# Second input projection: twelve of its fourteen tiles as six pairs of seven half-size products

## The chip, the cores and the metric

The kernel runs on one core of a Trainium2 chip. The metric is the device time of one execution in microseconds (us). The engines are PE (TensorE: matmuls), DVE (VectorE), ACT (ScalarE), POOL (GpSimd) and SP (SyncE, which here only starts DMA transfers). Each works through its own list of instructions in order, and they wait for one another by semaphores.

## The reference, cut to what matters

A first block (gated convolutions, a feed-forward part) turns `x`, 1024 tokens by 1024 channels, into the input of a second block. This one projects the normalised input `h` to 1984 columns `u`, and these feed a latent attention and a multiscale pool:

```python
h = _rms(x, norm_g[l]) * (1.0 + scale[:, None, :]) + shift[:, None, :]
hc = _rms(ctx, norm_g[l]) * (1.0 + scale_c) + shift_c
u = h @ w_in[l]            # 1024 x 1984
uc = hc @ w_in[l]
...
cq = u[..., OFF_CQ:OFF_CKV]        # 256 columns
ckv = u[..., OFF_CKV:OFF_KR]       # 128
k_rope = u[..., OFF_KR:OFF_GA]     # 64
gate_a = u[..., OFF_GA:OFF_PIN]    # 512
pool_in = u[..., OFF_PIN:OFF_GP]   # 512
gate_p = u[..., OFF_GP:D_IN_PROJ]  # 512
...
br_a = jax.nn.silu(gate_a) * mla_out
br_p = jax.nn.silu(gate_p) * _multiscale_pool(pool_in, w_pool, pool_scale)
y = jnp.concatenate([br_a, br_p], axis=-1) @ w_out[l]
```

`_multiscale_pool` takes four groups of 128 channels with windows of 2, 4, 8 and 16 tokens: window mean minus the value, times a 128x128 matrix per group (`w_pool`), times `pool_scale`. The attention has four heads; `cq` and `ckv` are normalised over their columns before they are expanded into queries, keys and values.

## The kernel before

Every float32 matmul is made as three products of shorter operands: each factor is split into a high part and the low rest, and high·high, high·low and low·high are summed. For weights, the high copy comes from ACT or POOL and the rest from a POOL subtraction; for the activations, ACT writes `XBh` (`xb_hi` in the rows) and DVE `XBl` (`xb_lo`).

A plain `gemm` (L963) of a column tile of 128 has 8 slices of the inner dimension, 3 products and 2 halves of 512 tokens: 48 matmuls 128x512. The second input projection uses it for its 14 full tiles after the key columns. The first input projection (L1108), the up-projection (L1251) and the output (L1638) already use another scheme: a pair of tiles, cut into halves in all three dimensions, is computed by seven products of half size instead of eight, with sums and differences of weight quarters and of token quarters as operands. One product has 4 slices times 3 products: 12 matmuls of 128x512. In the up-projection the rows call the token combinations `tok_comb`, the weight sums `w_sums` (DVE), the high copies `whi` (ACT, L1956) and the low parts `wlo` (POOL, L879). In the output, ACT copies a product's bank (`out_copies`, L2270) and DVE adds another to it (L3199).

The order on PE in the stage: context keys and rotary keys; keys (`key_tile`, interleaved with the DVE loop that makes `hT` and `XBl`, while ACT makes `XBh`, L2091); two query tiles; four tiles of gate a, with `row_sums` of the squared keys (L1029) inside the second and `column_sums` of the squared queries (L1020) inside the fourth; four tiles of pool input (`pin`); then four times a tile of gate p and a pooled product with `w_pool` (6 matmuls); then the heads (L1399 on). ACT evicts each tile (squares and copies of the queries L2104 and L2105, SiLU of the gates L2115 and L2129) and builds the scales with a logarithm and an exponential (L1711, L1717), each behind a table load. DVE writes the block's residual `y` (8 pieces; SP stores them to DRAM as `y_scratch`), the low parts of keys and queries, the rotary keys, and the pool sums (L2982 to L2997); a helper `pool_low` writes the low half of a pooled operand. ACT starts four DMAs that swap rotary halves (`U3`).

The lists of instructions are fixed in the program; no planner rearranges them.

## Time and profile before

| | |
|---|---|
| median of 3 runs | 1904.87 us (1903.58 to 1905.76) |
| profiled execution, span of the trace | 1904.2 us |
| granted TensorE clock over the span, share of full | 0.998 |
| PE busy | 1864.6 us (98%), 8807 matmul instructions |
| DVE / ACT / POOL busy | 1397.6 / 733.7 / 906.7 us |
| DMA | 166.63 MB, 88 GB/s on average |

The profiled execution has one span, which is compared with spans; the runs are timed without a profile. "Busy" is time in which an engine executes; matmuls are pipelined, so a busy PE can still be slower than its best. The positions in the rows are microseconds from the start of the span.

### The profile page before, as it was taken

To read this page: it belongs to the slowest core of one execution; us is meant where nothing else is said; L and a number is where in the kernel's file an instruction comes from. 1 tells how busy PE (TensorE), PEld (TensorE's weight loads), DVE (VectorE), ACT (ScalarE), POOL (GpSimd) and SP (SyncE) were. 2 spreads that over 40 slices of the span, in tenths; PEclk is the share of its full clock that TensorE was granted. 3 is DMA by queue.
4 is the path that set the end of the run, shared out by engine and by line. 5 is a ranking of instruction groups with operands and counts; after the bars stand their busy time and mean duration, and the time that the engine had idled before them with its cause. 6 is when DMAs were issued, how large, how long until landed. Compare 5 with 4: busy or idle time off the path is not lost.

```text
span 1904.2 us, 23795 instructions
## 1 busy us (share of the span) xinstructions
PE 1864.6 (98%) x8807; PEld 1544.8 (81%) x8807; DVE 1397.6 (73%) x1423; ACT 733.7 (39%) x990; POOL 906.7 (48%) x632
## 2 busy tenths in 40 slices
PE   7999999999999999999999999999999999999998
PEld 6788888778888888888887788878788878888887
DVE  7989988667348889898989786574633846667683
ACT  5433344441225333333341200243433236766643
POOL 5866766533334555555566555332233521222462
PEclk9999999999999999999999999999999999999999
DMA  4112234356112323232336435111123210000052
GB/s 164 52 45 89 67 111 144 122 177 187 45 45 66 100 67 99 66 99 66 99 136 232 146 106 198 56 41 38 45 82 112 84 45 1 12 12 1 1 177 67
DMA packets 190952, 166.63 MB, mean 88 GB/s; under 512 B 11267, under 2 KB 168912, under 8 KB 190864
## 3 DMA queue, kind: packets, MB, share of 16 engines
q1 hardware_dynamic: 189536, 162.82, 27.0%
...
## 4 chain that ended last, share of the span: by engine, by line
PE 84%; DVE 8%; ACT 3%; issue 2%; DMA 1%; POOL 1%; ACTq 0%; SPq 0%; DVEq 0%
PE ps L963 33%; PE ps L1251 19%; PE ps L1108 16%; PE ps L1638 3%; PE ps L1454 2%; PE ps L1489 1%; PE ps L1487 1%; PE ps L1488 1%; PE ps L1468 1%; PE ps L1465 1%; PE ps L1471 1%; PE ps L1474 1%; PE ps L1462 1%; DVE resid L2707 1%; DVE mod_acc L2410 1%
## 5 line engine op out<-in xcount | busy, mean ns | idle before, releaser
L833 POOL TENSOR_TENSOR small<-ones 128x1 f32<-128x1 f32 x75 | 22.2, 296 | 479.0 <-PE ps L963 438.7
L963 PE MATMUL ps<-xb_hi,whi 128*128 128x512 f32 x752 | 244.6, 393 | 5.1 <-DVE resid L2707 2.3
L963 PE MATMUL ps<-xb_lo,whi 128*128 128x512 f32 x752 | 242.2, 389 | 0.0
L963 PE MATMUL ps<-xb_hi,wlo 128*128 128x512 f32 x752 | 242.0, 389 | 0.0
L838 POOL TENSOR_TENSOR wlo<-raw,whi 128x1024 fp32r<-128x1024 f32 (+1 forms) x72 | 197.4, 2742 | 6.0
L879 POOL TENSOR_TENSOR wlo<-w_sums,whi 128x512 fp32r<-128x512 f32 x80 | 138.1, 1745 | 82.3 <-ACT whi L1956 82.3
L963 PEld LDWEIGHTS ps<-xb_hi,whi 128*128 128x128 f32 x752 | 140.2, 188 | 38.0 <-DVE resid L2707 3.1
L963 PEld LDWEIGHTS ps<-xb_lo,whi 128*128 128x128 f32 x752 | 141.2, 188 | 29.7 <-issue 0.2
L963 PEld LDWEIGHTS ps<-xb_hi,wlo 128*128 128x128 f32 x752 | 141.2, 188 | 29.6
L2390 DVE SCALAR_TENSOR_TENSOR ps<-glu_pad,tab,ps 128x1024 f32<-128x1024 f32 x116 | 149.2, 1286 | 2.9
L933 POOL TENSOR_SCALAR prob<-prob,small 128x512 f32<-128x512 f32 x64 | 50.5, 802 | 180.8 <-DVE small L3045 180.2
L1251 PE MATMUL ps<-tok_comb_hi,whi 128*128 128x512 f32 x320 | 124.5, 389 | 0.0
L1251 PE MATMUL ps<-tok_comb_lo,whi 128*128 128x512 f32 x320 | 124.5, 389 | 0.0
L1251 PE MATMUL ps<-tok_comb_hi,wlo 128*128 128x512 f32 x320 | 124.5, 389 | 0.0
L858 POOL TENSOR_TENSOR wlo<-w_in_sums,whi 128x512 fp32r<-128x512 f32 x64 | 88.2, 1381 | 58.5 <-ACT whi L1803 58.5
L963 PE MATMUL ps<-xa_hi,whi 128*128 128x512 f32 x352 | 113.5, 396 | 1.7 <-DVE resid L2707 0.8
L963 PE MATMUL ps<-xa_lo,whi 128*128 128x512 f32 x352 | 111.2, 390 | 0.0
L963 PE MATMUL ps<-xa_hi,wlo 128*128 128x512 f32 x352 | 111.1, 390 | 0.0
L1108 PE MATMUL ps<-xb_hi,whi 128*128 128x512 f32 x272 | 106.3, 391 | 1.5 <-DVE xb_lo L2424 0.9
L1108 PE MATMUL ps<-xb_hi,wlo 128*128 128x512 f32 x272 | 105.8, 389 | 0.0
L1108 PE MATMUL ps<-xb_lo,whi 128*128 128x512 f32 x272 | 105.8, 389 | 0.0
L2707 DVE TENSOR_TENSOR resid<-ps,resid 128x1024 f32<-128x1024 f32 x48 | 58.5, 1219 | 55.7 <-PE ps L963 55.6
...
## 6 DMA issues: line engine op xcount, KB each, us to landing
...
```

Source lines behind the costliest of these rows:

```text
L833: nc.gpsimd.tensor_tensor(small[:, 106 + slab.slot:107 + slab.slot], ones[:, 0:1], ones[:, 0:1], ALU.mult)
L838: nc.gpsimd.tensor_tensor(lo, src, f32(hi), ALU.subtract).then_inc(split_done, 1)
L858: nc.gpsimd.tensor_tensor(wlo[:, slot, cols], win_source(p, k), f32(whi[:, slot, cols]), ALU.subtract).then_inc(sem("win_split"), 1)
L879: nc.gpsimd.tensor_tensor(wlo[:, s, cols], comb_source(u, n), f32(whi[:, s, cols]), ALU.subtract).then_inc(sem("st_split"), 1)
L933: nc.gpsimd.tensor_scalar(Pr[t % 2][:, k], Pr[t % 2][:, k], rsum4[:, t % 4:t % 4 + 1], 0.0, ALU.mult, ALU.add).then_inc(sem("p_scaled"), 1)
L963: ins = mm(dst[j], w, r[j], start=first and f, stop=last and l)
L1108: last = mm(o, wp[:, slot, w], bp[:, k0 + j, c0:c0 + H], start=k in (1, 2, 5) and j == 0 and i == 0, stop=j == 3 and i == 2, skip_group_ch ...
L1251: last = mm(o, wp[:, s, w], bp[:, k, :], start=k == 0 and i == 0, stop=k == 3 and i == 2)
L1454: last = nc.tensor.transpose(PS[:, o:o + P], Pr[a][:, k * P:(k + 1) * P], ident[:, :])
L1638: last = mm(o, wp[:, slot, w], bp[:, k0 + j, c0:c0 + H], start=k in (1, 2, 5) and j == 0 and i == 0, stop=j == 3 and i == 2, skip_group_ch ...
L2390: stt(conv_ps if k < TAPS_A - 1 else conv[:, i, :], source, col("conv_a_w", i + 4 * k), conv_ps, ALU.mult, ALU.add).then_inc(sem("conv_tap ...
L2707: tt(R[:, m, :], pair(J), R[:, m, :], ALU.add).then_inc(*one(free(J)))
```

## The change

Two tiles of the pool input (pooling groups 3 and 2) stay plain gemms. The other twelve are made as six pairs of seven products: pair 0 the two other pool-input tiles, 1 and 2 gate a, 3 the queries, 4 and 5 gate p. `UP_AT` is the order of the 42 products; product 1 of the next pair stands between product 7 and product 4 of a pair. The weights go through a ring of four half slots: ACT's high copy (`u_hi`) waits for the product four earlier, POOL's subtraction (`u_split`) for the copy.

Around it work is dealt anew. ACT also writes `hfull`, the full-precision activations (8 copies in the h loop), from which DVE makes four token combinations in place and, with ACT's high copies (`comb_hi`), their low parts (`comb_low`). Rotary keys and the low part of `KSQ` move from DVE to POOL; the `U3` DMAs move from ACT's queue to SP's. `row_sums` moves into the first remaining pool-input tile, `column_sums` behind product (4,7). The four pooled products stand behind the products in `POOLED_AFTER`; ACT scales their results, and they are stored to DRAM and read back (`pool_results`). The gates of pairs 1 and 2 are stored and read back as `ga` (2 MB) at the end. The slabs, jobs and buffers of the old order are replaced, among them the mean and scale helpers. VectorE waits for all y stores (`y_out`) before it zeroes the pads of the pool buffers. The pooled branch ends with `branch_gate`, `branch_high` and `branch_low`, two of each per gate pair; those of pair 5 come in head 0.

```diff
+NUP = 6
+UP_AT = {(0, 1): 0}
+for _p in range(NUP):
+    for _k in (2, 6, 5, 7):
+        UP_AT[_p, _k] = len(UP_AT)
+    if _p + 1 < NUP:
+        UP_AT[_p + 1, 1] = len(UP_AT)
+    for _k in (4, 3):
+        UP_AT[_p, _k] = len(UP_AT)
+UP_PRODUCTS = len(UP_AT)
+UP_OF = {g: pk for pk, g in UP_AT.items()}
+PIN_PAIR, CQ_PAIR = 0, 3
+GATE_P = {4: (2, 3), 5: (0, 1)}
+POOLED_AFTER = {(1, 5): 0, (1, 3): 1, (2, 3): 2, (3, 7): 3}
...
+        JK = Lin(JOBS["mla_in"] + 3)
+        sp.wait_ge(sem("rbc_ready"), 5)
+        sp.dma_start(inv[:, :], A["inv_cnt"][GROUPS[0]:GROUPS[0] + 1, :].to_broadcast([P, S])).then_inc(sem("inv_in"), 16)
+        sp.wait_ge(*free(JK))
+        for half in (0, 32):
+            for u in range(2):
+                sp.dma_start(U3[ROPE + half + 16 * u:ROPE + half + 16 * (u + 1), 0:S],
+                             krT[half + 16 * (1 - u):half + 16 * (2 - u), 0:S]).then_inc(sem("rope_in"), 16)
...
         for m in range(8):
+            if m == 4:
+                sp.wait_ge(split_done, SLABS["pin"] + 2)
+                u_load(0)
             sp.wait_ge(sem("y_ready"), m + 1)
             sp.dma_start(ydram[m], R[:, m, :]).then_inc(sem("y_out"), 16)
-        L = Lin(SLABS["pin"])
-        for n, gq in enumerate(GROUPS):
-            slab8(L + n, w2, OFF_PIN + gq * P)
...
-        for n, gq in enumerate(GROUPS):
-            slab8(Lin(SLABS["pool"] + n), w2, OFF_GP + gq * P)
+        sp.wait_ge(job_done, JOBS["pin"] + 2)
+        u_load(1)
...
+        sp.wait_ge(*on("u_done", UP_AT[NUP - 1, 7] + 1))
+        sp.wait_ge(*on("ga_out", 64))
+        sp.dma_start(ga[:, :, :], gdram[0:4].rearrange("t p n -> p t n")).then_inc(sem("ga_in"), 16)
+        sp.wait_ge(*on("u_done", UP_PRODUCTS))
         sp.dma_start(csq[:, :], A["rope_q"]).then_inc(sem("rope_in"), 16)
...
+                pool.wait_ge(sem("rope_in"), 96)
+                nc.gpsimd.tensor_tensor(ktmp[:, :], U3[ROPE:P, 0:S], cossin[ROPE:P, :], ALU.mult).then_inc(sem("krot_mul"), 1)
+                pool.wait_ge(sem("krot_mul"), 1)
+                nc.gpsimd.tensor_tensor(krT[:, 0:S], krT[:, 0:S], cossin[0:ROPE, :], ALU.mult).then_inc(sem("krot_done"), 1)
+                pool.wait_ge(sem("krot_done"), 1)
+                nc.gpsimd.tensor_tensor(krT[:, 0:S], krT[:, 0:S], ktmp[:, :], ALU.add).then_inc(sem("krot_done"), 1)
+                for g in range(UP_PRODUCTS):
+                    slot, cols = u_ring(g)
+                    pool.wait_ge(*on("u_hi", g + 1))
+                    nc.gpsimd.tensor_tensor(wlo[:, slot, cols], u_source(*UP_OF[g]), f32(whi[:, slot, cols]),
+                                            ALU.subtract).then_inc(sem("u_split"), 1)
+                    if UP_OF[g] == (0, 7):
+                        pool.wait_ge(*on("u_split", g + 1))
+                        pool.wait_ge(sem("ksq_hi"), 1)
+                        nc.gpsimd.tensor_tensor(KSQ[ROPE:P, :], sqkr[:, :], f32(KSQ[0:ROPE, :]), ALU.subtract).then_inc(sem("ksq_low"), 1)
+                        pool.wait_ge(*on("ksq_low", 1))
...
             if n == 2:
+                pe.wait_ge(*free(Lin(JOBS["mla_in"] + 3)))
+                row_sums(sqck, NKEY, sem("lora_sq"), 3, SQ_AT)
...
+        J = Lin(JOBS["pin"])
+        L = Lin(SLABS["pin"])
+        gemm(J, L, XBh, XBl, KD, w8, between=lora_sums)
+        pe.wait_ge(sem("ck_f"), 1)
+        gemm(J + 1, L + 1, XBh, XBl, KD, w8)
+
+        def u_product(p, k):
+
+            g, o = UP_AT[p, k], u_bank(p, k)
+            slot, cols = u_ring(g)
+            pe.wait_ge(*on("u_split", g + 1))
+            if p == 0 and k in HX:
+                pe.wait_ge(*on("hx_dve", 4 + HX_LOW.index(k) + 1))
+            if (p, k) == (0, 1):
+                pe.wait_ge(*free(J))
+            if (p, k) == (0, 5):
+                pe.wait_ge(*free(J + 1))
+            if k == 1 and p >= 2:
+                pe.wait_ge(*on("u_act", up_acts(p - 2, 1)))
+            if k == 2 and p >= 2:
+                pe.wait_ge(*on("u_add", 3 * p - 5))
+            if k == 5 and p >= 2:
+                pe.wait_ge(*on("u_add", 3 * p - 3))
+            if k in (6, 7, 4):
+                pe.wait_ge(*on("u_copy", 3 * p + {6: 1, 7: 2, 4: 3}[k]))
+            if k == 3:
+                pe.wait_ge(*on("u_add", 3 * p + 2))
...
+            last.then_inc(sem("u_done"), 1)
+
+        for p, k in UP_AT:
+            u_product(p, k)
+            if (p, k) in POOLED_AFTER:
+                pooled_product(POOLED_AFTER[p, k])
+            if (p, k) == (4, 7):
+                pe.wait_ge(*on("wp_read", 4))
+                column_sums(pres[0], 8, 16, sem("s12_done"), 23)
...
+        pe.wait_ge(*on("u_add", 3 * NUP - 3))
+        pe.wait_ge(*on("u_act", up_acts(NUP - 2, 1)))
...
+            fn(hfull[:, m, :], hT[:, m, :], ACT.Identity, bias=mod_sb[:, m, 0:1]).then_inc(sem("h_hi"), 1)
+        row_log(rbc, D, 6, 0, S, at_col=6 * H)
+        row_scale(PS[:, 6 * H:6 * H + S], rbc[:, :]).then_inc(sem("rbc_ready"), 1)
+
+        def comb_hi(k):
+
+            b, k0, c0 = HX[k]
+            act.wait_ge(*on("hx_dve", HX_ORDER.index(k) + 1))
+            fn(xch[:, b, :, :], hfull[:, k0:k0 + 4, c0:c0 + H], ACT.Copy).then_inc(sem("hx_hi"), 1)
+
         keys_out(J + 2, 0, S)
+        comb_hi(5)
         rope_out(J + 3, 0, S)
-        act.wait_ge(*free(J + 3))
-        for half in (0, 32):
-            for u in range(2):
-                act.dma_start(U3[half + 16 * u:half + 16 * (u + 1), 0:S],
-                              krT[half + 16 * (1 - u):half + 16 * (2 - u), 0:S]).then_inc(sem("rope_in"), 16)
...
+        row_log(sqck, 128, 7, 0, NKEY, at_col=SQ_AT)
+        row_scale(PS[:, SQ_AT:SQ_AT + NKEY], sqck[:, :]).then_inc(sem("rbc_ready"), 1)
...
+        def u_hi(g):
+
+            if g >= UP_PRODUCTS:
+                return
+            p, k = UP_OF[g]
+            slot, cols = u_ring(g)
+            if g < 4:
+                act.wait_ge(job_done, JOBS["pin"] + 1 + g // 2)
+            else:
+                act.wait_ge(*on("u_done", g - 2 if g in (UP_PRODUCTS - 3, UP_PRODUCTS - 1) else g - 3))
+            if k in (1, 2, 4):
+                u_raw_in(act, p)
+            else:
+                act.wait_ge(*on("u_sum", 4 * p + {5: 1, 6: 2, 7: 3, 3: 4}[k]))
+            fn(whi[:, slot, cols], u_source(p, k), ACT.Copy).then_inc(sem("u_hi"), 1)
+
+        def u_copy(p, n):
+
+            k, to = ((1, upc[p % 2][:, 0:H]), (6, upc[p % 2][:, H:S]), (7, upd[p % 2][:, H:S]))[n]
+            if n == 0 and p in (3, 4):
+                act.wait_ge(*on("ga_out", 32 * (p - 2)))
+            elif n == 0 and p == 5:
+                act.wait_ge(sem("cq_lo"), 2)
+                act.wait_ge(sem("lora_sq"), 6)
...
+            act.wait_ge(*on("u_done", UP_AT[p, k] + 1))
+            fn(to, u_bank(p, k), ACT.Copy).then_inc(sem("u_copy"), 1)
...
+        for p in range(NUP):
+            b = 7 * p + 1
+            if p:
+                u_hi(b + 4)
+                if p == 3:
+                    pooled_high(3)
+                if p == 5:
+                    root(8, 1)
+                u_copy(p, 1)
+            u_hi(b + 5)
+            u_hi(b + 6)
+            if p == 1:
+                pooled_out(0)
+            u_copy(p, 2)
+            if p == 3:
+                pooled_out(3)
+            u_hi(b + 7)
+            if p in (1, 2):
+                pooled_high(p)
+                inverse_counts(p + 1)
+                if p == 1:
+                    pool_in(3)
+            if p + 1 < NUP:
+                u_copy(p + 1, 0)
+                u_hi(b + 8)
+                u_hi(b + 9)
             else:
...
+                branch_high(4, 0)
+                branch_high(4, 1)
+            u_last_block(p)
+            u_hi(b + 10)
+            if p in (1, 2):
+                pooled_out(p)
+            if p == 4:
+                act.wait_ge(*on("wp_out", 64))
+                fn(CKh[:, :], ckf[:, :], ACT.Copy).then_inc(sem("ck_hi"), 1)
+            if p:
+                u_finish(p)
+            else:
+                pooled_high(0)
+                inverse_counts(1)
+                pool_in(2)
...
-                dve.wait_ge(sem("h_hi"), m)
+                dve.wait_ge(sem("h_hi"), 2 * m)
...
+        u_sums(0, (1,))
+        combination(3)
+        comb_low(6)
+        comb_low(5)
+        u_sums(0, (3,))
+        comb_low(7)
+        comb_low(4)
...
+        pool_sums(0, 0, 3)
+        for p in range(NUP):
+            u_add(p, upc[p % 2][:, 0:H], 2, 1)
+            if p == 1:
+                pool_sums(1, 2, 3)
+                pool_means(1)
+            if p == 4:
+                for k in (1, 0):
+                    dve.wait_ge(*on("u_act", up_acts(CQ_PAIR, 3 - k)))
+                    stt(CQl[:, k, :], (upc, upd)[k][CQ_PAIR % 2][:, :], col("q_lora_g_2", k), f32(CQh[:, k, :]),
+                        ALU.mult, ALU.subtract).then_inc(sem("cq_lo"), 1)
+                dve.wait_ge(sem("lora_sq"), 6)
+                tt(pres[0][:, :], pres[0][:, :], pres[1][:, :], ALU.add).then_inc(sem("s12_done"), 1)
+            if p == 5:
+                rstd(8, 256, 1, 1, at_col=16, to=rql)
+                branch_gate(4, 0)
+                branch_gate(4, 1)
+            u_add(p, upd[p % 2][:, H:S], 5, 3)
+            u_sums(p + 1, (1,))
+            if p == 0:
+                pool_sums(0, 3, 4)
+                pool_means(0)
+            if p == 5:
+                dve.wait_ge(sem("ck_hi"), 2)
+                tt(CKl[:, :], ckf[:, :], f32(CKh[:, :]), ALU.subtract).then_inc(sem("ck_lo"), 1)
+                branch_low(4, 0)
+                branch_low(4, 1)
+            if p in (1, 2, 3):
+                pool_low(p)
+            u_add(p, upc[p % 2][:, H:S], 3, 2)
+            u_sums(p + 1, (3,))
+            if p == 0:
+                pool_low(0)
+                pool_sums(1, 0, 2)
+            if p in (1, 2):
+                pool_sums(p + 1, 0, GROUPS[p + 1] + 1)
+                pool_means(p + 1)
+        branch_gate(5, 0)
+        branch_gate(5, 1)
...
-                pool_low(3)
+                branch_low(5, 0)
+                branch_low(5, 1)
```

## Rows read from the trace of the kernel before

**Rows 1.** Busy time by stretch: PE, PEld, DVE, ACT, POOL, clock, DMA, GB/s
```profile
594.00:990.00 396.00, 396.00 (x1749) 328.01 (x1748) 354.28 (x346) 144.37 (x203) 228.10 (x144) 1.00 0.28 86
1393.00:1558.00 165.00, 163.97 (x724) 133.89 (x723) 78.25 (x56) 40.93 (x39) 65.48 (x49) 1.00 0.29 86
1558.00:1580.00 22.00, 19.68 (x103) 15.35 (x102) 16.79 (x22) 20.76 (x29) 2.48 (x3) 1.00 0.22 55
```

**Rows 2.** Timeline of PE: start, us, engine, line, operation, tiles
```profile
1393.84 0.70 PE L963 MATMUL ps<-xb_hi,whi 128*128 128x512 f32 x2
...
1429.32 2.31 PE L1029 MATMUL ps<-sq_ckv,ones 128*128 128x512 f32 x6
...
1457.75 1.84 PE L1020 MATMUL ps<-ones,sq_cq 128*128 128x1 f32 x16
...
1557.63 0.47 PE L1399 MATMUL ps<-ck_hi,whi 128*128 128x512 f32 x1
```

**Rows 3.** Timeline of ACT, evictions of two tiles (in brackets, idle before)
```profile
1405.04 1.03 ACT L2104 ACTIVATE sq_cq<-ps 128x1024 f32<-128x1024 f32 x1 [9.20 <-PE ps L963]
...
1415.92 1.03 ACT L2104 ACTIVATE sq_cq<-ps 128x1024 f32<-128x1024 f32 x1 [8.94 <-PE ps L963]
```

**Rows 4.** Waits of PE's weight loads, 1390 to 1560: us in total, times, longest
```profile
PEld ps L963 <- ACT silu_gate_p L2129: 1.6, 3, 1.3
```

**Rows 5.** Chain of waits, 1550 to 1582: start, us, what ran
```profile
1556.35 1.03 ACT silu_gate_p L2129
...
1559.85 0.70 ACT kn_hi L2179
...
1579.27 0.50 PE ps L1462
```

**Rows 6.** Operations by tile: shortest/median/longest ns, first to last start in us
```profile
L2645 DVE TENSOR_TENSOR tok_comb<-tok_comb x4: 2292/2948/4308, 575.3 to 593.8; 128x2048 f32<-128x2048 f32 x4
...
L1942 ACT ACTIVATE tok_comb_hi<-tok_comb x4: 1898/1910/1923, 587.2 to 597.1; 128x2048 fp32r<-128x2048 f32 x4
...
L1956 ACT ACTIVATE whi<-w_sums x80: 612/632/635, 608.6 to 979.1; 128x512 fp32r<-128x512 f32 x80
...
L879 POOL TENSOR_TENSOR wlo<-w_sums,whi x80: 1286/1650/2336, 609.3 to 980.2; 128x512 fp32r<-128x512 f32 x80
...
L2691 DVE TENSOR_TENSOR w_sums<-raw x10: 692/1477/1479, 607.1 to 947.5; 128x512 f32<-128x512 f32 x10
...
L2270 ACT ACTIVATE out_copies<-ps x9: 597/598/602, 1836.3 to 1889.2; 128x512 f32<-128x512 f32 x9
...
L3199 DVE TENSOR_TENSOR out_copies<-ps,out_copies x9: 676/684/693, 1847.6 to 1896.6; 128x512 f32<-128x512 f32 x9
...
L2091 ACT ACTIVATE xb_hi<-h_t,mod_sb x8: 1150/1154/1158, 1368.1 to 1383.7; 128x1024 fp32r<-128x1024 f32 x8
```

**Rows 7.** Timeline of ACT, a table load and the operation that it serves
```profile
1440.89 1.28 ACT L1711 ACT_TABLE_LOAD   x1
1442.19 1.33 ACT L1711 ACTIVATE sq_ckv<-ps,small 128x1280 f32<-128x1280 f32 x1
```

**Rows 8.** DMA, 1380 to 1450: GB/s in 40 equal slices
```profile
GB/s 0 0 0 0 0 0 0 0 65 263 108 190 124 0 9 0 0 155 145 0 0 0 0 4 146 405 424 417 414 419 419 324 35 0 0 0 5 0 147 152
```

**Rows 9.** Timeline of DVE around 1501
```profile
1500.45 1.22 DVE L2997 TENSOR_TENSOR xa_lo<-pooled,xa_hi 128x1024 fp32r<-128x1024 f32 x1 [1.13 <-ACT xa_hi L2134]
1501.59 3.43 DVE L2982 TENSOR_TENSOR win_a<-u_pad 128x1039 f32<-128x1039 f32 x1
```

**Rows 10.** Timeline of POOL: one beside that addition, one that began first
```profile
1500.48 3.45 POOL L838 TENSOR_TENSOR wlo<-raw,whi 128x1024 fp32r<-128x1024 f32 x1
...
1534.76 2.40 POOL L838 TENSOR_TENSOR wlo<-raw,whi 128x1024 fp32r<-128x1024 f32 x1
```

**Rows 11.** Timeline of PE near the start of the program
```profile
17.29 1.94 PE L1038 MATMUL ps<-ident,x_scaled 128*128 128x128 f32 x8 [2.35 <-DVE x_scaled L2363]
```

**Rows 12.** Busy time near the start, columns as in rows 1
```profile
17.00:21.00 4.00, 3.71 (x19) 3.71 (x20) 3.52 (x7) 2.97 (x6) 0.00 (x0) 0.57 0.33 130
```

More of the change, by code:

```diff
@@ L56 @@
 for _name, _n in (("glu", 2), ("mix_b", KD // 2), ("mix_a", KD // 2), ("wo", KD),
-                  ("ffn", 4), ("down", 4 * (NDC - 1) + 2), ("ple", KD), ("mla_in", 4), ("ga", 4),
-                  ("pin", 4), ("w_pool", 2), ("pool", 4), ("heads", HEADS), ("out", 2), ("end", 0)):
+                  ("ffn", 4), ("down", 4 * (NDC - 1) + 2), ("ple", KD), ("mla_in", 2),
+                  ("pin", 2), ("heads", HEADS), ("out", 2), ("end", 0)):
     SLABS[_name] = _at
@@ new lines, in u_load, with ga_store @@
+        def u_load(p):
+            first, second = up_columns(p)
+            for r in range(4):
+                c = (first, second)[r // 2]
+                sp.dma_start(u_raw(p, r).rearrange("p (k n) -> p k n", n=P),
+                             w2[H * (r % 2):H * (r % 2 + 1), c:c + P].rearrange("(k p) n -> p k n", p=P)
+                             ).then_inc(sem(f"u_raw{p % 2}"), 16)
+        def ga_store(p):
+            sp.wait_ge(*on("u_act", up_acts(p, 2)))
+            sp.dma_start(gdram[2 * p - 1], upd[p % 2][:, :]).then_inc(sem("ga_out"), 16)
+            sp.wait_ge(*on("u_act", up_acts(p, 3)))
+            sp.dma_start(gdram[2 * p - 2], upc[p % 2][:, :]).then_inc(sem("ga_out"), 16)
@@ L1385, in tensor_program @@
-        gemm(j + 2, L + 2, XBh, XBl, KD, w8)
-        gemm(j + 3, L + 3, XBh, XBl, KD, w8, between=lora_scales)
-        J, L = Lin(JOBS["pin"]), Lin(SLABS["pin"])
-        for gq in range(4):
-            gemm(J + gq, L + gq, XBh, XBl, KD, w8, begins=3 if gq == 2 else 1)
-        J, L = Lin(JOBS["pool"]), Lin(SLABS["pool"])
-        for n, gq in enumerate(GROUPS):
-            gemm(J + 2 * n, L + n, XBh, XBl, KD, w8)
-            pe.wait_ge(sem("branch2_lo"), n + 1)
-            gemm(J + (2 * n + 1), None, XAh[:, 4 + gq:5 + gq, :], XAl[:, 4 + gq:5 + gq, :], 1,
-                 lambda k: (gq, slice(0, P)), new_slab=False, weights=(wpoolh, wpooll))
+                pe.wait_ge(*free(Lin(JOBS["mla_in"] + 3)))
@@ new lines, in u_sums @@
+        def u_sums(p, which):
+            if p >= NUP:
+                return
+            a11, a12, a21, a22 = (u_raw(p, r) for r in range(4))
+            s1, s2, s3, s4 = (u_sum(p, r) for r in range(4))
+            if 1 in which:
+                u_raw_in(dve, p)
+                if p >= 2:
+                    dve.wait_ge(*on("u_split", UP_AT[p - 1, 5] + 1))
+                tt(s1, a21, a22, ALU.add).then_inc(sem("u_sum"), 1)
+                dve.wait_ge(*on("u_sum", 4 * p + 1))
+                tt(s2, s1, a11, ALU.subtract).then_inc(sem("u_sum"), 1)
+            if 3 in which:
+                if p:
+                    dve.wait_ge(*on("u_split", UP_AT[p - 1, 3] + 1))
+                else:
+                    dve.wait_ge(job_done, JOBS["pin"] + 2)
+                tt(s3, a11, a21, ALU.subtract).then_inc(sem("u_sum"), 1)
+                dve.wait_ge(*on("u_sum", 4 * p + 2))
+                tt(s4, a12, s2, ALU.subtract).then_inc(sem("u_sum"), 1)
@@ new lines, in pool_sums @@
+        def pool_sums(n, first, last):
+            u = upad[n % 2]
+            if first == 0:
+                if n:
+                    dve.wait_ge(sem("branch2_lo"), n)
+                if n < 2:
+                    dve.wait_ge(*free(Lin(JOBS["pin"] + n)))
+                else:
+                    dve.wait_ge(*on("u_pin", n - 1))
+            for s in range(first, last):
+                src, dst = u if s == 0 else (wB, wA)[s % 2], (wA, wB)[s % 2]
+                ln = TB // 4 - (1 << (s + 1)) + 1
```

413 lines of the change are left out of this document (253 added, 160 removed).

## The prediction, made before the changed kernel was run

> **What bounds the kernel now.** I read the stretches by engine first. In the stage that the change rewrites TensorE is busy for 163.97 of 165 us, while VectorE has work for 78, ScalarE for 41 and GpSimd for 65 [rows 1]. The up-projection, which already runs seven-product pairs, is bound by TensorE too: 396.00 of 396.00, beside VectorE at 354 and GpSimd at 228 [rows 1]. That row matters twice: it shows that the scheme can hide its helpers, and how much VectorE work that can mean.
>
> Then TensorE's own order of time [rows 2]. The stage runs from 1393.84 (first query gemm) to 1557.63 (first product of the heads), 163.8 us. A plain tile is the distance between two evictions that each wait for a gemm, 1415.92−1405.04 = 10.88 us [rows 3], so one of its 48 matmuls takes 0.2267. Fourteen tiles are 152.3, the four pooled products of six matmuls 4×1.36 = 5.4, row sums 2.31 and column sums 1.84 [rows 2]: 161.9. The other 1.9 us are waits; the list of waits puts 1.6 us of it on the pooled branch's SiLU [rows 4].
>
> Behind the stage, the chain of waits leaves TensorE: from 1556.35 to 1579.27 it runs through ScalarE and VectorE [rows 5], and ScalarE is busy for 20.76 of these 22 us [rows 1]. A delay of head 0's first inputs is paid in full.
>
> **The change part by part.**
>
> *TensorE's work.* Twelve tiles go (130.6 us), 42 products of twelve matmuls come (42×2.72 = 114.2). Row sums, column sums and pooled products stay. **−16.3.** The waits of the old order go with it: **−1.9** (bounds −1.9 and 0).
>
> *Entry.* ScalarE gets eight more copies (hfull) in the loop over m. The two ScalarE operations take 2×1.15 plus about 0.04 of handoff = 2.34 per m; the loop now advances every 2.23 (1368.1 to 1383.7, seven steps) [rows 6]. The copy before XBl's wait also delays XBl of m = 0 by 1.15, some of which the key tiles were already waiting for. I take **+0.8**, seven times the 0.11; bounds 0.3 and 1.5.
>
> *Row sums moved forward.* In the first remaining tile (pin 0) they wait for rope_out on ScalarE, which now stands behind the longer h loop, two log/exp steps with a 1.28 us table load each [rows 7], the key outputs and one comb_hi of 1.9 [rows 6]. Added up from the before-trace's positions: done about 1398.3; TensorE is there at 1397.3. **+1.0** (0.5 to 1.5). Then the row scale is ready about 1407.6, before pin 0 ends at 1408.6: no second wait.
>
> *Pairs 0 to 2.* Pair 0 starts when pin 1 ends, near 1419.5. It needs token combinations and their low halves from VectorE, which first waits until all eight y stores have landed. 4 MB at 419 GB/s is 10 us [rows 8]; starting about 1400, behind the rotary copies now on SP, they land near 1415.5. VectorE then does two weight sums, combination 3 and the lows, to about 1422.4, 1425.2, 1429.8 and 1432.5; products 6, 5, 7 and 4 are due at 1425.0, 1427.7, 1430.4 and 1435.8. So all are in time with at least 0.6 to spare for product 7, and y landing has about 2.5 us of slack before anything is late. Small waits for product 3's sum and two pooled products: 0.2+0.6+0.5 = **+1.3**, bounds 0 and 6. Here the row that speaks against the change is that of VectorE and GpSimd together: an addition of 1.2 us took 3.43 beside a GpSimd subtraction that took 3.45 instead of 2.40 [rows 9, 10], that is, they ran one after the other. Fully serial, the stretch costs 9.1 us more (a rival below); I stay near the low end because the up-projection has the same mix of engines without a wait of TensorE [rows 1]. The Trainium skill, page "GPSIMD Engine Reference", section "8. Key points", states that GpSimd shares its SBUF interfaces with VectorE, with contention when a VectorE instruction has two SBUF inputs; by that rule the serial sum holds wherever both are queued, and these two rows agree with it.
>
> *Pooled product 3.* It stands right after (3,7) and needs pool_low(3). On VectorE that is behind u_add(3,5), which needs ScalarE's copy of product 7's bank, taken after (3,7) ends, and behind two weight sums. So TensorE waits: drain 0.16, copy 0.60, add 0.68, two sums at 0.69, pool_low 1.22, three handoffs of 0.06: 0.16+0.60+0.68+1.38+1.22+0.18 = **+4.2** [rows 6, 9]. If the two sums meet GpSimd they take 1.48 each [rows 6]: 5.8; below, 3.9 if drain and handoffs vanish.
>
> *Last pair.* No product of a next pair lies between (5,7) and (5,4). (5,7) waits for a copy that on ScalarE stands behind the CKh copy, pair 4's SiLUs, a weight copy and a square-root table load of 1.28 [rows 7]; (5,4) waits for drain, copy and handoff (0.16+0.60+0.12 = 0.9 [rows 6]). **+1.8** (0.9 to 2.5).
>
> *Head 0's entry.* Before, the last SiLU (1.03) began 1.28 ahead of the first head product and KNh began 2.22 after it [rows 2, 5]. Now the last product is followed by drain 0.16, add 0.68, SiLU 1.03, the two KRs copies 2.45 and four handoffs of 0.05: KNh at +4.5, so 2.3 later. On VectorE there is also one more pool low-half (1.2 [rows 9]) in this chain; the second high-half copy runs while VectorE leads. **+3.5** (2.3 to 5).
>
> *Costed at nothing.* Weight loads of 256 KB: 419 GB/s [rows 8] brings a pair's 1 MB in 2.5 us of its 19. Storing the gates and reloading 2 MB at the end: 5 us, and the first use is some 7 us after the last product; without that cover it costs what is late. KSQ and rotary operations on GpSimd: 7 splits of 1.3 to 1.65 per pair [rows 6] leave it over 7 of 19 us; uncovered, each is a delay of the ring. Squares and CQl of pair 3 are done about 1.8 us before the column sums need them.
>
> Sum: −16.3 −1.9 +0.8 +1.0 +1.3 +4.2 +1.8 +3.5 = −5.6. The profiled span of 1904.2 becomes 1898.6. The median of the runs is 1904.87, 0.7 above that span; I carry this over: **1899.3**. All low bounds together give −9.3, all high bounds +6.0.
>
> **Rivals.**
>
> *Serial VectorE and GpSimd.* Suppose that no VectorE operation overlaps a GpSimd one. From the y landing to pooled product 0 (due about 1449.5) VectorE has a combination and four lows of 128x2048 at no less than 2.3 (11.5), four sums at 0.69 (2.8), nine pool operations at 1.22 (11.0) and three adds at 0.68 (2.0): 27.3 [rows 6, 9]. GpSimd has seven splits at 1.29 (9.0) and, estimated by element count from these, 5 for KSQ and w_pool: 14.0. That is 41.3 in 34.1 us: +7.2. Pair 1: eight pool operations, four sums, three adds and seven splits make 23.6 against seven products and a pooled one, 20.4: +3.2. Of these 10.4, 1.3 is counted: 1899.3+9.1 = 1908.4. For: the two rows [rows 9, 10]. Against: the up-projection [rows 1], and that much of this work is needed later than it is queued.
>
> *The clock falls at pooled product 3.* Early in the program TensorE idled 2.35 us [rows 11], and over the next 4 us the granted clock was 0.57 [rows 12], near the lower of its two levels (1.2 of 2.4 GHz): 0.43×4 = 1.7 us lost. The wait of 4.2 is longer than that gap: 1901.0. Against: this gap followed no long busy stretch. The Trainium skill, page "TensorE: Matmul & The Clock Gate", section "HAM oscillation — how this bites in real kernels", has the clock fall in idle gaps between groups of matmuls; rows 12 agree.
>
> *The ring starves: slower.* With four half slots, a weight copy waits for the product four back, and ScalarE takes its work strictly in order, so a copy stuck behind a SiLU or a branch wait holds the next product. 42 products: 0.13 us each takes the whole gain, 0.22 each makes it slower by over 0.2%. One product's time lost in each pair is 6×2.72 = 16.3: 1915.6. For: ScalarE's queue here carries pool inputs, gates and pooled results that the up-projection's lacks. Against: a copy of 0.63 per 2.72 us product [rows 6] leaves three products of lead.
>
> *The waits are hidden.* If VectorE runs ahead of this count at pooled product 3 (−4.2) and the tail copies are early (−1.8): 1893.3.
>
> **How the numbers follow.** A measurement here tells about 0.2% from no change, 3.8 us. Chances: the forecast 0.50 (its own range 1895.6 to 1904), serial 0.15, clock 0.13, ring 0.08, hidden 0.14. Faster by over 0.2% means under 1901.1: 0.36 of the forecast, half the clock's (0.06), all of hidden (0.14): 0.56. Slower means over 1908.7: 0.04 of the forecast, 0.08 of serial, 0.01 of clock, 0.07 of ring: 0.20. Same: 0.24. The range goes from 1893 (hidden) to 1909 (just past serial); ring and the edges lie outside, about 0.2.
>
> **What would show it.** Right: products 2.72 apart in the pairs; one wait of about 4 us before the pooled product behind (3,7), released by VectorE; waits near 0.9 at (5,7) and (5,4); KNh 4 to 5 us after the first head product; y landed near 1415.5. Wrong: weight-load waits on GpSimd's splits throughout (ring), VectorE additions of 3 us in pairs 0 and 1 (serial), a granted clock below 1 in pair 4 (clock), y landing after 1418 (each further us costs one), or a chain in head 0 that hides the late KNh.

## The result, and the profile after

The changed kernel takes 1910.88 us (median of 8 runs, 1909.24 to 1912.34); the kernel before took 1905.22 beside it. The ratio is 1.003, 95% interval 1.002 to 1.004: slower by 5.7 us, where 5.6 us faster was forecast, and just above the range (1909). The profiled execution has a span of 1910.2 us, 6.0 above that of before, so it shows the loss. TensorE executes 72 matmuls fewer, as the change says.

The stretches first (columns as in [rows 1]):

```profile
1393.00:1558.00 165.00, 153.09 (x653) 123.25 (x652) 119.77 (x95) 84.02 (x110) 98.78 (x54) 0.97 0.40 127
1420.00:1445.00 25.00, 19.10 (x71) 14.37 (x70) 24.86 (x14) 10.97 (x15) 21.20 (x9) 0.86 0.19 53
1558.00:1580.00 22.00, 17.45 (x80) 13.35 (x80) 20.43 (x22) 19.68 (x26) 3.30 (x3) 0.95 0.41 127
```

TensorE is busy for 153 of these 165 us instead of 164. About half of what is missing lies in the 25 us of pair 0, where VectorE is busy throughout (24.86) and GpSimd nearly so (21.20), and where the granted clock is 0.86. TensorE's own waits, from its timeline (start, us, engine, line, operation; in brackets the idle time before and who ended it):

```profile
1397.47 2.40 PE L1171 MATMUL ps<-sq_ckv,ones 128*128 128x512 f32 x6
...
1427.59 0.47 PE L1565 MATMUL ps<-h_comb_hi,whi 128*128 128x512 f32 x1 [0.29 <-issue]
...
1432.08 0.50 PE L1565 MATMUL ps<-h_comb_hi,whi 128*128 128x512 f32 x1 [1.49 <-POOL wlo L1055]
...
1439.21 0.79 PE L1565 MATMUL ps<-xb_hi,whi 128*128 128x512 f32 x1 [4.12 <-POOL wlo L1055]
...
1468.63 0.47 PE L1565 MATMUL ps<-xb_hi,whi 128*128 128x512 f32 x1 [0.78 <-DVE u_second L3351]
...
1508.26 0.70 PE L1105 MATMUL ps<-pooled_hi,w_pool_hi 128*128 128x512 f32 x2 [3.92 <-issue]
...
1549.19 0.47 PE L1565 MATMUL ps<-h_comb_hi,whi 128*128 128x512 f32 x1 [0.54 <-ACT u_first L2355]
...
1552.93 0.47 PE L1565 MATMUL ps<-h_comb_hi,whi 128*128 128x512 f32 x1 [0.78 <-ACT u_second L2355]
...
1558.50 0.39 PE L1578 MATMUL ps<-ck_hi,whi 128*128 128x512 f32 x1
```

The last row is the first product of the heads, at 1557.63 before [rows 2]. The first remaining pool-input tile begins at 1394.75, so the stage takes 163.75 us, where its old form takes 163.79 from the first query gemm: the work that TensorE saves is lost again in the stage. The waits stand before products (0,5), (0,7) and (1,1), product (1,3), pooled product 3, and (5,7) and (5,4) of the last pair. The granted clock behind the two long ones, and in head 0 (0.50 is the lower of its two levels, 1.2 of 2.4 GHz):

```profile
1437.00:1439.00 2.00, 0.00 (x0) 0.00 (x0) 1.97 (x2) 0.00 (x0) 1.98 (x1) 0.66 0.00 0
1439.00:1444.00 5.00, 4.79 (x11) 3.79 (x12) 4.93 (x5) 0.00 (x0) 4.92 (x4) 0.50 0.00 0
1509.00:1513.00 4.00, 4.00 (x12) 3.09 (x11) 0.00 (x0) 1.74 (x2) 0.41 (x1) 0.57 0.20 81
1576.00:1582.00 6.00, 4.72 (x26) 4.60 (x26) 3.26 (x6) 5.97 (x9) 0.00 (x0) 0.72 0.00 0
```

So each of the two long waits is paid again: 0.50×5 = 2.5 us behind the one of 4.12, 0.43×4 = 1.7 behind the one of 3.92. In head 0 the fall costs nothing that the profile shows: ScalarE and VectorE lead there. Two rows of ScalarE, before and after:

```profile
1571.17 1.47 ACT L2215 ACTIVATE k_scale_bc<-ps,small 128x256 f32<-128x256 f32 x2
```

```profile
1575.76 1.47 ACT L2508 ACTIVATE k_scale_bc<-ps,small 128x256 f32<-128x256 f32 x2
```

This operation begins 13.54 us behind the first head product before and 17.26 after, 3.72 later. The first turned probabilities come 28.89 behind it before (at 1586.52) and 32.61 after (at 1591.11), also 3.72 later. So the whole delay is there before the clock falls, at about 1577.

What makes pair 0 wait is seen where VectorE and GpSimd are put side by side. First VectorE, then GpSimd, timelines:

```profile
1420.81 6.68 DVE L3262 TENSOR_TENSOR xa_lo<-h_full,h_comb_hi 128x2048 fp32r<-128x2048 f32 x2
1427.42 0.68 DVE L3288 TENSOR_TENSOR w_sums<-raw 128x512 f32<-128x512 f32 x1
...
1428.62 5.55 DVE L3262 TENSOR_TENSOR xa_lo<-h_full,h_comb_hi 128x2048 fp32r<-128x2048 f32 x2
1434.10 3.94 DVE L3306 TENSOR_TENSOR win_a<-u_pad 128x1039 f32<-128x1039 f32 x1
1438.07 2.18 DVE L3306 TENSOR_TENSOR win_b<-win_a 128x1037 f32<-128x1037 f32 x1
```

```profile
1419.68 5.66 POOL L1055 TENSOR_TENSOR wlo<-u_sums,whi 128x512 fp32r<-128x512 f32 x2 [4.00 <-ACT whi L2338]
1428.90 3.13 POOL L1055 TENSOR_TENSOR wlo<-w_sums,whi 128x512 fp32r<-128x512 f32 x1 [3.56 <-ACT whi L2338]
1432.10 4.84 POOL L1060 TENSOR_TENSOR k_rope_squares<-sq_kr,k_rope_squares 64x1280 fp32r<-64x1280 f32 x1
1437.02 2.14 POOL L1055 TENSOR_TENSOR wlo<-w_raw,whi 128x512 fp32r<-128x512 f32 x1
```

Two splits that take 1.29 each at their shortest [rows 6] take 5.66 together beside low halves; the low halves, 2.28 at their shortest, take 6.68 for two. The rotary squares, 2.92 where they begin first (e5), take 4.84: they end 2.8 us after the last low half, which ends at 1434.17. The addition at 1434.10, 1.2 alone [rows 9], takes 3.94: it ends 1.1 us after the rotary squares end at 1436.94. GpSimd's list has the split of (0,7), the rotary squares and the split of (1,1) one behind the other, and that is the wait of 4.12. The busy columns contain this waiting of one engine for the other; the rows show it as length and not as idle time. An addition of VectorE with one operand in PSUM (the memory of the matmul results, `ps` in the rows) does not wait in this way. Two of VectorE, then one of GpSimd:

```profile
1443.12 0.68 DVE L3351 TENSOR_TENSOR u_second<-ps,u_second 128x512 f32<-128x512 f32 x1
1443.72 1.15 DVE L3280 TENSOR_TENSOR w_sums<-w_raw 128x512 f32<-128x512 f32 x1
```

```profile
1443.04 1.28 POOL L1066 TENSOR_TENSOR w_pool_lo<-w_pool_raw,w_pool_hi 128x512 fp32r<-128x512 f32 x1
```

The first has one operand in PSUM and keeps its 0.68 beside GpSimd's 1.28. The weight sum has both in SBUF, the on-chip memory of the other tiles; it takes 1.15 and ends 0.55 after GpSimd's operation, which ends at 1444.32.

### The profile page after: what moved, and what is told of

Its sections match the earlier page's. It is cut to its first block, busy times and chain, and to the rows that moved or that the text cites. A ratio compares the mean times of both kernels' runs of the same rounds, so it can differ in the third digit from the quotient of the medians.

```text
span 1910.2 us, 23874 instructions
## 1 busy us (share of the span) xinstructions
PE 1857.0 (97%) x8735; PEld 1536.5 (80%) x8735; DVE 1447.6 (76%) x1466; ACT 787.0 (41%) x1071; POOL 936.4 (49%) x637
## 4 chain that ended last, share of the span: by engine, by line
PE 83%; DVE 9%; issue 3%; ACT 2%; DMA 1%; POOL 1%; SPq 0%; ACTq 0%; DVEq 0%; POOLq 0%
PE ps L1105 28%; PE ps L1393 19%; PE ps L1250 16%; PE ps L1565 4%; PE ps L1820 3%; PE ps L1634 2%; PE ps L1667 1%; PE ps L1669 1%; PE ps L1668 1%; PE ps L1642 1%; PE ps L1645 1%; PE ps L1648 1%; PE ps L1654 1%; PE ps L1651 1%; DVE resid L3000 1%
## 5 line engine op out<-in xcount | busy, mean ns | idle before, releaser
L957 POOL TENSOR_TENSOR small<-ones 128x1 f32<-128x1 f32 x61 | 15.6, 255 | 387.0 <-PE ps L1105 354.2
L1105 PE MATMUL ps<-xb_hi,whi 128*128 128x512 f32 x560 | 185.0, 393 | 4.9 <-DVE resid L3000 2.3
L1105 PE MATMUL ps<-xb_lo,whi 128*128 128x512 f32 x560 | 183.0, 389 | 0.0
L1105 PE MATMUL ps<-xb_hi,wlo 128*128 128x512 f32 x560 | 182.9, 389 | 0.0
L962 POOL TENSOR_TENSOR wlo<-raw,whi 128x1024 fp32r<-128x1024 f32 (+2 forms) x59 | 161.8, 2742 | 4.9
L1105 PEld LDWEIGHTS ps<-xb_hi,whi 128*128 128x128 f32 x560 | 104.5, 188 | 29.4 <-issue 3.7
L1105 PEld LDWEIGHTS ps<-xb_lo,whi 128*128 128x128 f32 x560 | 105.1, 188 | 22.2 <-issue 0.2
L1105 PEld LDWEIGHTS ps<-xb_hi,wlo 128*128 128x128 f32 x560 | 105.1, 188 | 22.0
L982 POOL TENSOR_TENSOR wlo<-w_in_sums,whi 128x512 fp32r<-128x512 f32 x64 | 88.2, 1380 | 59.2 <-ACT whi L1985 59.2
L1250 PE MATMUL ps<-xb_hi,whi 128*128 128x512 f32 x272 | 106.3, 391 | 0.9 <-DVE xb_lo L2717 0.9
L1250 PE MATMUL ps<-xb_hi,wlo 128*128 128x512 f32 x272 | 105.8, 389 | 0.0
L1250 PE MATMUL ps<-xb_lo,whi 128*128 128x512 f32 x272 | 105.8, 389 | 0.0
```

The lines of the kernel that those rows point to most:

```text
L962: nc.gpsimd.tensor_tensor(lo, src, f32(hi), ALU.subtract).then_inc(split_done, 1)
L982: nc.gpsimd.tensor_tensor(wlo[:, slot, cols], win_source(p, k), f32(whi[:, slot, cols]), ALU.subtract).then_inc(sem("win_split"), 1)
L1105: ins = mm(dst[j], w, r[j], start=first and f, stop=last and l)
L1250: last = mm(o, wp[:, slot, w], bp[:, k0 + j, c0:c0 + H], start=k in (1, 2, 5) and j == 0 and i == 0, stop=j == 3 and i == 2, skip_group_ch ...
```

## Experiments

Ratios are to the kernel before, run beside each; the changed kernel's own is 1.003. An interval is 0.001 to 0.0015 (1.9 to 2.9 us) to either side. In profiles I compare the stretch from the row sums to the first head product: what lies ahead of the stage moves by up to 3.7 us from one profile to the next, without a change there.

### e1: rotary squares earlier on GpSimd

```diff
         comb_hi(6)
+        act.wait_ge(sem("krot_done"), 2)
+        act.wait_ge(sem("lora_sq"), 4)
+        fn(KSQ[0:ROPE, :], sqkr[:, :], ACT.Copy).then_inc(sem("ksq_hi"), 1)
         pool_in(0)
...
-                    if UP_OF[g] == (0, 7):
+                    if UP_OF[g] == (0, 2):
```

> Edit: the rotary squares' high copy on ScalarE moves up behind the third token copy, and GpSimd's low half of it from behind the split of product (0,7) to behind the split of (0,2), where GpSimd has 4 us without work. Theory (a long operation in the split queue at the wrong place): the 4.12 us wait of TensorE before product (1,1) goes, and with it the stretch of half clock behind it (about 2.5 us); a wait of about 0.5 us for product (0,3) takes part of it back. Total about -6 us against the changed kernel's 1910.9, so near 1905. Rival (VectorE and GpSimd share what they read through and are simply full in pair 0): the wait only moves to (0,7) or (0,3), and the total falls by less than 2 us.

Measured: 1909.37 us, 1.0018 (1.0009 to 1.0027), so about 0.12% or 2.3 us below the changed kernel. The wait of 4.12 is gone, but others have come:

```profile
1426.26 0.47 PE L1565 MATMUL ps<-h_comb_hi,whi 128*128 128x512 f32 x1 [2.04 <-issue]
...
1434.04 0.50 PE L1565 MATMUL ps<-h_comb_hi,whi 128*128 128x512 f32 x1 [1.49 <-POOL wlo L1055]
...
1444.61 0.50 PE L1565 MATMUL ps<-xb_hi,whi 128*128 128x512 f32 x1 [1.52 <-POOL wlo L1055]
...
1456.89 0.71 PE L1105 MATMUL ps<-pooled_hi,w_pool_hi 128*128 128x512 f32 x2 [1.10 <-issue]
```

With three smaller ones the waits of pairs 0 and 1 are 7.8 us in sum, against 6.7 before the edit. My theory of a wrong place falls: moving the operation moves the wait. What is gained is the clock, 1.00 from 1425 to 1470; no single wait there is longer than 2.04. From row sums to the first head product the profile gains only 0.4 us (160.6 instead of 161.0), so how much the edit gains is not clear.

### e2: the low half of pooled operand 3 earlier on VectorE

```diff
+            if p == 3:
+                pool_low(3)
             u_add(p, upd[p % 2][:, H:S], 5, 3)
             u_sums(p + 1, (1,))
...
-            if p in (1, 2, 3):
+            if p in (1, 2):
                 pool_low(p)
```

> Edit: on VectorE the low half of pooled operand 3 moves ahead of the addition that needs the bank of product (3,7) and of the two weight sums behind it. Theory: the 3.92 us wait of TensorE before pooled product 3 goes, and the stretch of half clock that follows it (0.50 to 0.66 for 3.4 us, about 1.6 us lost) goes with it: -5.5 us, near 1905.4. Rival (the clock there fell for another reason than this wait): -3.9 us, and the clock at pair 4 still falls.

Measured: 1903.93 us, 0.9995 (0.9986 to 1.0004). The wait is gone and the clock stays at 1.00 from 1500 to 1520. From row sums to the first head product the profile has 155.5 us instead of 161.0: 5.5 us, the wait and the clock. (The ratios differ by 0.35%, 6.7 us, the same within their intervals.)

### e3: the fourth combination ahead of the wait for the y stores

```diff
         combination(1)
         combination(2)
+        combination(3)
...
         u_sums(0, (1,))
-        combination(3)
         comb_low(6)
```

> Edit: VectorE's fourth token combination moves ahead of its wait for the y stores, into 2.7 us in which it waits. Theory: VectorE is 2.2 us earlier in pair 0, so the 1.49 us wait before (0,7) goes; the rotary squares begin by as much earlier on GpSimd, and the wait before (1,1) shrinks from 4.12 to about 2.5, perhaps short enough for the clock to stay: -3 us, or -5.5 with the clock. Rival (GpSimd alone sets pair 0): no more than -0.5 us.

Measured: 1909.65 us, 1.0019 (1.001 to 1.0028): 2.1 us less. The wait before (0,7) is gone, as the theory says; that before (1,1) is 4.08, hardly shorter, and the clock falls behind it as before. In the profile this stretch gains 0.9 us, less than either the theory's 3 or the difference of the ratios.

### e4: the three together

> The three edits together. Theory: -6 and -5.5 and, of the third, the 1.5 us before (0,7): -13 us against the changed kernel, near 1898, 0.35% faster than the kernel before. Rival (VectorE and GpSimd full in pair 0): only the second edit counts fully, near 1903 to 1905.

Measured: 1902.67 us, 0.9983 (0.9974 to 0.9992): 9 us below the changed kernel, and faster than the kernel before. Row sums to first head product: 153.4 us. The parts do not add up to the theory's 13: 6.4 us of short waits remain in pairs 0 and 1, none over 1.54, and the clock is 1.00 from 1420 to 1470.

### e5: half of the combinations' low parts left out

```diff
-            tt(XAl[:, k0:k0 + 4, c0:c0 + H], hfull[:, k0:k0 + 4, c0:c0 + H], f32(xch[:, b, :, :]), ALU.subtract).then_inc(sem("hx_dve"), 1)
+            tt(XAl[:, k0:k0 + 2, c0:c0 + H], hfull[:, k0:k0 + 2, c0:c0 + H], f32(xch[:, b, 0:2, :]), ALU.subtract)
+            nc.vector.memset(f32(XAl[:, k0 + 2:k0 + 4, c0:c0 + H]), 0.0).then_inc(sem("hx_dve"), 1)
```

> Edit on top of the kernel with the three edits: each low half of a token combination is made for two of its four slices, and the other two are filled with zeros, so half of the low parts of the four combinations is left out. The work of GpSimd and the order of everything stay. Theory (operations of VectorE with two operands in SBUF and GpSimd's run one after the other): some 4 us less in the shared stretch, GpSimd's splits of pair 0 come near their undisturbed 1.3 us, and the waits of TensorE in pairs 0 and 1, 6.4 us in sum with the three edits, fall to about 3: -3 us against that kernel. Rival (the place of operations in the queues alone sets the waits): the splits keep their 2 to 3 us and the time falls by less than 1 us.

Measured: 1897.75 us, 0.9955 (0.9941 to 0.997), about 5 us below e4; from row sums to the first head product the profile has 149.7 us instead of 153.4. Waits of pairs 0 and 1: 0.81+0.78+1.08+1.07 = 3.7 instead of 6.4. Three rows of VectorE and two of GpSimd from this run:

```profile
1416.34 3.18 DVE L3282 TENSOR_TENSOR u_sums<-raw 128x512 f32<-128x512 f32 x1
...
1420.16 1.22 DVE L3263 TENSOR_TENSOR xa_lo<-h_full,h_comb_hi 128x1024 fp32r<-128x1024 f32 x1
1421.54 0.91 DVE L3264 MEMSET xa_lo<- 128x1024 f32 x1 [0.16 <-issue]
```

```profile
1416.05 2.92 POOL L1060 TENSOR_TENSOR k_rope_squares<-sq_kr,k_rope_squares 64x1280 fp32r<-64x1280 f32 x1
1421.11 3.67 POOL L1055 TENSOR_TENSOR wlo<-u_sums,whi 128x512 fp32r<-128x512 f32 x2 [2.14 <-ACT whi L2338]
```

A weight sum of 0.68 us takes 3.18 when the rotary squares are ahead of it: it ends 0.55 after they do. With GpSimd's work unchanged its splits are shorter (two in 3.67 instead of 5.77 in e4), and so are the waits. They do not come down to 1.3 each, as I had expected; half of the subtractions is still there. VectorE's own time is not what is saved: subtraction, gap and filling take 1.22+0.16+0.91 = 2.3 us, as long as an undisturbed low half (2.28). What is halved is the time in which VectorE reads two operands from SBUF. So it is these reads, in which one of the two engines waits for the other, and not the places in the queues that set pair 0.

### e6: pool work later

```diff
-                    if UP_OF[g] == (0, 4):
+                    if UP_OF[g] == (0, 3):
...
-        pool_sums(0, 0, 3)
...
-                pool_sums(0, 3, 4)
+                pool_sums(0, 0, 4)
```

> Edit on top of the three: GpSimd splits w_pool behind the split of product (0,3) instead of before it, and VectorE makes the first pool sums behind the additions of products 2 and 5 and two weight sums of the next pair instead of before them. Theory: the 1.53 us wait before (0,3), where the w_pool split stood in GpSimd's queue, goes, and the weight sums of pair 1 come 5 us earlier: -1.5 to -2 us. Against it, the pooled product 0 may come up to 2 us late, since the same work lies before it: rival, 0 to +1 us, with the wait now before pooled product 0.

Measured: 1902.85 us, 0.9985 (0.9976 to 0.9994), as e4. The wait before (0,3) went, the one at pooled product 0 grew from 1.10 to 2.76, with a clock of 0.83 from 1450 to 1460: the rival.

### e7: head 0 in a new order, and e8: all of it

```diff
+        act.wait_ge(*on("u_done", UP_PRODUCTS))
         for v in range(2):
             fn(KRs[ROPE * v:ROPE * (v + 1), :], krot[:, :], ACT.Copy).then_inc(sem("kr_hi"), 1)
...
                 branch_high(5, 0)
-                branch_high(5, 1)
+                act.wait_ge(*on("u_add", 3 * NUP))
+                fn(upc[1][:, :], upc[1][:, :], ACT.Silu).then_inc(sem("u_act"), 1)
...
             query_fold(0)
+            if h == 0:
+                branch_gate(5, 1)
+                branch_low(5, 0)
```

> Edit on top of the three: behind the last product ScalarE copies the rotary keys first, and the SiLU of the last gate block, its product with the pooled result and the two low halves of pair 5 move to where ScalarE and VectorE wait later in head 0. Theory (a chain through ScalarE and VectorE sets head 0, so that what is taken out of it counts in full): 1.7 us for the addition and SiLU ahead of the rotary keys and 2.3 us for the two low halves: -3 to -4 us. Rival (the chain has a parallel one close behind, through TensorE and the tables of ScalarE): -1 us or less.

Measured: 1904.53 us, 0.9991 (0.998 to 1.0002): no gain over e4 (head 0's entry takes 32.5 us in the profile, 32.6 in e4). The chain of waits names what took its place: the query table's load, behind the gates' 2 MB, and the moved products, now ahead of the values' low parts.

```profile
1549.69 6.34 DMA cos_sin_q<-in_rope_q
1556.06 0.76 DVE cos_sin_q L3479
1556.85 1.50 DVE kr_lo_lo L3481
...
1567.18 1.23 DVE u_first L3344
1568.40 1.14 DVE xa_lo L3351
1569.54 1.81 DVE v_lo L3509 x3
```

e8 has the edits of e6 and e7 on top of e4.

> The three edits, the later pool work and the new order of head 0 together. Theory: the sum of the parts, -5 us against the kernel with three edits, near 1898, 0.4% faster than the kernel before. Rival: the pool work gives nothing, near 1899.5.

Measured: 1904.38 us, 0.9989 (0.9977 to 1.0), with both of these flaws and clocks of 0.73 and 0.76 from 1570 to 1590.

### e9: the same with the table's load early

```diff
+        sp.wait_ge(*on("wp_done", 4))
+        sp.dma_start(csq[:, :], A["rope_q"]).then_inc(sem("rope_in"), 16)
         sp.wait_ge(*on("ga_out", 64))
         sp.dma_start(ga[:, :, :], gdram[0:4].rearrange("t p n -> p t n")).then_inc(sem("ga_in"), 16)
...
+                act.wait_ge(*on("u_add", 3 * NUP))
+                fn(upc[1][:, :], upc[1][:, :], ACT.Silu).then_inc(sem("u_act"), 1)
                 act.wait_ge(sem("kr_lo"), 1)
...
+            if h == 0:
+                branch_high(5, 0)
+                branch_high(5, 1)
             fn(sd[:, 12:13], ones[:, 0:1], ACT.Sqrt)
...
+                branch_gate(5, 1)
             query_lo(1)
```

> Edit on top of the three: the query table's load goes ahead of the 2 MB of gates instead of behind the last product; ScalarE copies the rotary keys before the last SiLU, and the high and low halves of pair 5 come at the end of head 0's entry, where ScalarE waited 2.8 us. In the first try at this (e7) the table landed 6.3 us after the last product and became the chain, and the low halves held up the values' low parts by 1.5 us. Theory: with these two gone the earlier rotary keys count: the time from the first head product to the first turned probabilities, 32.6 us with the three edits, falls to about 30: -2.5 us. Rival: the log, exponential and root tables of ScalarE set this stretch, -0.5 us or less.

Measured: 1897.67 us, 0.9957 (0.9943 to 0.9971), the best version: 8 us faster than before. From row sums to the first head product it takes 153.4 us, as e4. From the first head product to the first turned probabilities it takes 29.65 us, against 28.89 before and 32.6 in the changed kernel and in e4, and the clock there is 1.00:

```profile
1548.00:1580.00 32.00, 28.60 (x147) 22.02 (x147) 25.88 (x40) 28.50 (x39) 5.66 (x7) 1.00 0.30 95
```

### e10: pooled product 0 later as well

The edits are those of e9, this one, and the later split of w_pool as in e6:

```diff
-POOLED_AFTER = {(1, 5): 0, (1, 3): 1, (2, 3): 2, (3, 7): 3}
+POOLED_AFTER = {(1, 7): 0, (1, 3): 1, (2, 3): 2, (3, 7): 3}
```

> The edit of e9, and pooled product 0 behind (1,7) instead of (1,5), and the w_pool split behind that of (0,3). Theory: the 1.5 us wait before (0,3) and the 1.1 us wait before pooled product 0 go too: -5 us against the kernel with three edits, near 1898. Rival (shared reads of VectorE and GpSimd): only one of the two waits goes, -3.5 us.

Measured: 1900.27 us, 0.9969 (0.9958 to 0.9981): not better than e9, and 155.1 us from row sums to the first head product instead of 153.4. The two waits became one of 1.23 before (0,3), behind VectorE's addition, and one of 2.02 before (1,7), behind ScalarE's copy, with clocks of 0.93 and 0.90 after it (1450 to 1460 and 1460 to 1470).

### e11: TensorE kept busy ahead of pooled product 3

```diff
+            if n == 3:
+                for i in range(16):
+                    mm(PS[:, H * (6 + i % 2):H * (7 + i % 2)], wpoolh[:, gq, :], XBh[:, i % 8, 0:H], start=True, stop=True)
+                pe.wait_ge(sem("branch2_lo"), n + 1)
```

> Edit on the changed kernel: TensorE does 16 throwaway matmuls (3.6 us) into the two banks of pooled product 3 before it waits for its operand. The order and the work of the other engines stay. Theory (the clock falls because TensorE idles there): the wait is as long as before, but the granted clock stays at 1.00 after it: -1.6 us, near 1909.3. Rival (the clock falls for another reason, or its loss is not on the path): no change within 0.5 us.

Measured: 1908.1 us, 1.0013 (1.0004 to 1.0022), 0.17% below the changed kernel; from row sums to the first head product 159.7 instead of 161.0, 1.4 us. The wait is as long, filled:

```profile
1502.41 3.89 PE L1528 MATMUL ps<-xb_hi,w_pool_hi 128*128 128x512 f32 x16
1506.45 0.73 PE L1105 MATMUL ps<-pooled_hi,w_pool_hi 128*128 128x512 f32 x2
```

```profile
1501.00:1511.00 10.00, 9.86 (x43) 7.72 (x43) 3.12 (x4) 2.40 (x4) 1.45 (x2) 1.00 0.47 141
```

So the clock's fall behind this wait comes from the idle TensorE, and it costs about what the row said.

## Why the prediction was wrong

Term by term, in us of the profiled executions:

| step | forecast | profile after |
|---|---|---|
| products for tiles | −16.3 | −16.3 |
| old waits | −1.9 | −1.9 |
| entry | +0.8 | +0.8 |
| row sums | +1.0 | 0 |
| pairs 0 to 2 | +1.3 | 10.6: 6.7 of waits, 2.5 of clock, 1.4 of drains and slow first matmuls |
| pooled product 3 | +4.2 | 5.8: 3.9 of wait, 1.7 of clock, 0.2 of drain |
| last pair | +1.8 | 1.8: 1.3 of waits, the rest drains and slow first matmuls |
| head 0 | +3.5 | 3.7 |
| later | 0 | 1.4, beside a clock of 0.91 in head 2 |

The times of the pairs are what TensorE takes beyond 2.72 a product, 1.36 a pooled product and 1.84 for the column sums: 74.5 us instead of 63.9 from 1418.77 to 1493.29 (22 products, three pooled), 20.8 instead of 15.0 from there to 1514.06 (five, one pooled), 44.4 instead of 42.6 from there to 1558.50 (fifteen). A bracketed wait is shorter than the loss, for a matmul's row is 0.39 long where the next starts 0.23 behind it, and the first ones behind a wait are slow. The column makes +5.9; the spans differ by 6.0.

Right were the work, the entry (pin 0 begins at 1397.47−2.72 = 1394.75 instead of 1393.84 [rows 2]; 0.09 of the 0.91 lies ahead of the h loop, whose first copy starts at 1368.18 instead of 1368.09), the last pair, and the place and length of the wait at pooled product 3, which e2 removed. Head 0 is right in sum and make-up: KNh comes 4.81 us behind the first head product, 2.6 later than before (2.3 forecast), and one more low half on VectorE takes 1.1 (1.2 forecast). e9 shows that most of it was order and not work. The row sums found rope_out just done. The y stores landed near 1417.2 instead of 1415.5, within the slack that was counted; e3, in which VectorE no longer waits for them, gains 0.9 us. The 1.4 behind head 0 comes and goes between profiles: from the first turned probabilities to the end, 319.1 us here and 317.7 before, the edited kernels have the same program, and six of them (e2, e4, e5, e6, e9, e10) take 317.1 to 317.3, the other five 318.6 to 320.4.

**The step that failed is "Pairs 0 to 2", at +1.3 where the profile has 10.6**, and with it the rotary squares "costed at nothing". I had the rows that showed VectorE and GpSimd one after the other [rows 9, 10], summed the serial case, and put it aside because the up-projection has the same mix without a wait [rows 1]. It has not. There the combinations start from 575.3 to 593.8 and their low halves from 597.0 to 609.6. Of GpSimd's splits only the first two stand among them, and these too are long; the others come from 609.3 on [rows 6]. TensorE has other work meanwhile. The low halves, the two splits, and the stretch (columns as in [rows 1]) before:

```profile
L2772 DVE TENSOR_TENSOR tok_comb_lo<-tok_comb,tok_comb_hi x4: 2279/2826/3380, 597.0 to 609.6; 128x2048 fp32r<-128x2048 f32 x4
```

```profile
601.88 5.21 POOL L879 TENSOR_TENSOR wlo<-raw,whi 128x512 fp32r<-128x512 f32 x2 [6.93 <-ACT whi L1956]
```

```profile
594.00:610.00 16.00, 16.00 (x72) 13.28 (x71) 15.93 (x11) 5.28 (x5) 6.84 (x4) 1.00 0.31 98
```

In pair 0 five VectorE operations of 128x2048 and the pool sums stand between GpSimd's splits, and the rotary squares and w_pool stand in GpSimd's list besides. The rival of serial engines was the right one, as its sign in the prediction says (VectorE additions of 3 us: 3.94): in pair 0 the place in the queue matters little (e1 and e3 gain 0.4 and 0.9 us in the stretch), and e5 shows that the shared reading does. The Trainium skill, page "GPSIMD Engine Reference", section "8. Key points", states that GpSimd shares its SBUF interfaces with VectorE; the rows of pair 0 agree, with 3.94 us for an addition beside GpSimd's 4.84.

**Second, the rivals were taken as exclusive.** The clock's fall was priced rightly (1.7, measured 1.7 at that place), but as a case of its own with a chance of 0.13. It came on top of the others: behind the wait at pooled product 3, which was in the forecast itself, and behind the serial wait of 4.12. e11 shows for the first of these that TensorE's idling brings it. The Trainium skill, page "TensorE: Matmul & The Clock Gate", section "HAM oscillation — how this bites in real kernels", has the clock fall in gaps between matmul groups; the rows agree: 0.50 behind 4.12 us, 1.00 where the gap of 3.92 was filled (e11). The forecast's own wait, serial pair 0 and these clocks together would have been 1899.3+9.1+1.7+2.5 = 1912.6. That this is close to the 1910.88 measured is in part luck: pairs 0 to 2 cost 6.8 beyond the 1.3 without their clock, not 9.1, and 1.4 came behind head 0.

Why the run to run spread of e7 and e8 is wide (1899.65 to 1909.85 in e8), and why the clock in head 2 fell in some profiles and not in others, stays open. So does how much shorter the waits of pair 0 can be made with all the low parts kept.
